# One unit in place of eight for the compressed attention branch of a recurrent mixer

## The reference

```python
k_cmp = compress(kc, pe_k, ck1, ck2)          # gelu(blk @ w1) @ w2, 15 blocks
v_cmp = compress(vc, pe_v, cv1, cv2)
s = jnp.einsum('bqhgd,bhcd->bhgqc', qb, k_cmp)
s = s - slopes[None, :, :, None, None] * jnp.abs(t[:, None] - cmp_end[None, :])
ok_c = cmp_end[None, :] <= t[:, None]
p_c = jax.nn.softmax(jnp.where(ok_c, s, NEG), axis=-1) * jnp.any(ok_c, axis=-1)[:, None]
o_c = jnp.einsum('bhgqc,bhcd->bqhgd', p_c, v_cmp)
...
return gb[..., 0:1] * o_c + gb[..., 1:2] * o_s + gb[..., 2:3] * o_w
```

## Time and profile before

| what | value |
|---|---|
| median of three runs (lowest to highest) | 1489.45 us (1488.96 to 1489.46) |
| profiled execution: its time, its span | 1488.83 us, 1486.7 us |
| granted TensorE clock, mean over the span | 0.992 |
| the doubling loop, from its first P to the tail's first product | about 130.7 to 228.2 us |

### The profile page before, as it was taken

How to read it: one execution, slowest core, us unless ns; L and a number is a source line. 1 busy time by engine, 2 the same in 40 slices (tenths; PEclk the granted TensorE clock), 3 DMA queues, 4 the chain that set the end, 5 groups by cost and what they waited for, 6 DMA issues and landing times.

```text
span 1486.7 us, 26239 instructions
## 1 busy us (share of the span) xinstructions
PE 1450.2 (98%) x10328; PEld 1332.9 (90%) x10328; DVE 958.1 (64%) x1577; ACT 706.2 (48%) x1159; POOL 86.9 (6%) x130
## 2 busy tenths in 40 slices
PE   8999999999999999999999999999999999999997
PEld 7887988899998999989988999999999878899997
DVE  4765545776666866666557666676666666676665
ACT  6753443544335434446665434354443656444342
POOL 2040001000002000010000000000000114000000
PEclk9999989999999999999999999999999999999999
DMA  8343000555453645433335555445454424355440
GB/s 343 145 149 128 1 2 1 199 217 203 174 195 110 238 180 202 179 128 128 128 128 221 204 187 193 176 165 211 170 200 182 147 89 163 136 209 205 171 169 29
DMA packets 26576, 238.07 MB, mean 160 GB/s; under 512 B 2544, under 2 KB 6784, under 8 KB 7808
## 3 DMA queue, kind: packets, MB, share of 16 engines
q1 hardware_dynamic: 23968, 233.65, 42.2%
q10 hardware_dynamic: 2528, 3.32, 0.7%
HBM read 235.89 MB, written 1.07 MB: 159 GB/s over the span
## 4 chain that ended last, share of the span: by engine, by line
PE 90%; DVE 5%; ACT 3%; issue 2%; POOL 1%; DMA 0%; ACTq 0%; DVEq 0%; POOLq 0%
PE ps L435 87%; DVE w_gu L1919 1%; PE ps L816 1%; DVE uT_l L1876 1%; PE ps L895 1%; DVE ring_r L1912 0%; DVE x L1938 0%; PE ps L439 0%; DVE ring_r L2270 0%; ACT uT_h L1241 0%; PE ps L1022 0%; DMA cst<-consts_in 0%; ACT wk L1419 0%; POOL small L1766 0%; POOL small L1767 0%
## 5 line engine op out<-in xcount | busy, mean ns | idle before, releaser
L435 PE MATMUL ps<-uT_h,w_gu 128*128 128x256 f32 x3520 | 614.3, 280 | 0.3
L435 PEld LDWEIGHTS ps<-uT_h,w_gu 128*128 128x128 f32 x3520 | 537.8, 188 | 11.1 <-issue 1.6
L435 PE MATMUL ps<-uT_l,w_gu 128*128 128x256 f32 x1760 | 478.8, 279 | 0.0
L435 PE MATMUL ps<-w_dn,h_r 128*128 128x512 f32 x1320 | 326.2, 396 | 2.1 <-issue 1.0
L435 PEld LDWEIGHTS ps<-uT_l,w_gu 128*128 128x128 f32 x1760 | 325.5, 188 | 0.0
L435 PEld LDWEIGHTS ps<-w_dn,h_r 128*128 128x128 f32 x1320 | 239.4, 188 | 53.3 <-issue 3.7
L1288 ACT CAST w_gu<-ring 128x2048 fp32r<-128x2048 f32 x110 | 209.9, 1909 | 156.3 <-PE ps L435 155.4
L1919 DVE TENSOR_TENSOR w_gu<-ring,w_gu 128x2048 fp32r<-128x2048 f32 x110 | 252.1, 2292 | 35.3 <-ACT w_gu L1288 35.3
L1949 DVE TENSOR_TENSOR us<-ps,bc 128x256 f32<-128x256 f32 x110 | 46.5, 423 | 202.9 <-PE ps L435 202.8
L1301 ACT ACTIVATE wk<-wk 128x256 f32<-128x256 f32 x110 | 46.1, 419 | 260.3 <-DVE wk L1947 260.3
L1294 ACT CAST w_dn<-ring 128x1024 fp32r<-128x1024 f32 x110 | 115.7, 1052 | 82.6 <-PE ps L435 82.4
(11 more groups left out here) (370 smaller groups left out, 1843.5 us busy)
## 6 DMA issues: line engine op xcount, KB each, us to landing
ring<-wstream SPq DMA_DIRECT2D x144, 1536.0 KB, 6.5
cst<-consts_in SPq DMA_DIRECT2D x1, 2185.0 KB, 13.7
wk<-t_row ACTq DMA_DIRECT2D x1, 2048.0 KB, 8.6
wk<-masks_in SPq DMA_DIRECT2D x1, 1216.0 KB, 23.4
x<-x_in SPq DMA_DIRECT2D x2, 512.0 KB, 4.5
ring<-wstream SPq DMA_DIRECT2D x1, 1024.0 KB, 9.0
inh<-gains ACTq DMA_DIRECT2D x2, 512.0 KB, 9.7
out_dram<-x SPq DMA_DIRECT2D x4, 256.0 KB, 2.2
```

Source lines behind the costliest of these rows:

```text
L435: return pe.matmul(o, l, r, start=start, stop=stop, skip_group_check=True)
```

## The change

The eight compressed units of a token tile become one unit that holds all eight heads. So there are 34 units in place of 48, in the same six groups, of 8, 1, 8, 8, 1 and 8 (the last unit of each is in `NSA_LAST` = 7, 8, 16, 24, 25, 33). For the merged unit:

- PE makes the scores of the two groups by four products of 32 columns, one for each pair of heads (j, j + 4), each with other weights; one transpose of 128 by 128; and one value product of 512 columns against `Vbd`, a block-diagonal tile that DVE builds once in `compress()` from the compressed values and a mask.
- DVE makes four operations of 128 columns in place of the fused one: sum, maximum over 16, difference, product with the slopes; and two steps later a sum over 16 for the denominators.
- ACT makes one plain exponential of 128 columns and one copy.

The steps are spread anew: `NSA_STEPS` is 1 and 2 in turn for q = 2 to 21 and 1 for q = 22 and 23, and the first step of a q is now always the one between P and dM. DVE's result follows four steps behind a group's last unit, `if i - 4 in NSA_LAST` (it was five). ACT's and PE's waits on `o_ready` go by the group, `a["pos"] == 0 and a["grp"] >= 2`. DVE's `compress()` moves from q = 4 to q = 2, and the constants grow by 16 columns.

```diff
-        hid = sb("hid", [P, 2, 2, 48])
+        hid = sb("hid", [P, 2, 160])
+        hid_k, hid_v = hid[:, :, 0:32], hid[:, :, 32:160]
         kcT = sb("kcT", [P, 2, 16])
-        vc = sb("vc", [16, 2, HD])
+        Vbd = inh[:, 2 * D:2 * D + 512].rearrange("p (u n) -> p u n", n=HD)
+        cmp_max = small[:, 64:72]
...
-        NSA_STEPS, CMP_FROM, BRANCHES = [0, 0] + [2] * 20 + [3, 3], 6, (1, 0, 2)
+        NSA_STEPS, CMP_FROM, BRANCHES = [0, 0] + [1, 2] * 10 + [1, 1], 6, (1, 0, 2)
...
-                    for b in BRANCHES:
+                    for n, b in enumerate(BRANCHES):
+                        grp = 3 * t + n
+                        if b == 0:
+                            units.append(dict(cmp=True, q=[qT[:, j, tk] for j in range(4)], K=P, grp=grp, pos=0, last=True,
+                                              dist=C("alibi_cmp", 16 * t, 16 * t + 16)))
+                            continue
                         for h in range(8):
                             g, slope = h // 4, 2.0 ** -(h + 1)
-                            u = dict(q=qT[:, h % 4, tk], scale=slope)
-                            if b == 0:
-                                u.update(k=kcT[:, g, 0:NC_CMP], K=NC_CMP, v=[vc[0:NC_CMP, g, :]],
-                                         dist=C("alibi_cmp", 16 * t, 16 * t + NC_CMP))
-                            else:
-                                kx, o = (ksT, kwT)[b - 1], (b - 1) * P + g * HD
-                                u.update(k=kx[:, g, 0:K], K=K, v=[vsw[:, kt, o:o + HD] for kt in range(t + 1)],
-                                         dist=C("alibi", P * (1 - t), P * (1 - t) + K))
-                            units.append(u)
+                            kx, o = (ksT, kwT)[b - 1], (b - 1) * P + g * HD
+                            units.append(dict(cmp=False, q=qT[:, h % 4, tk], scale=slope, grp=grp, pos=h, last=h == 7,
+                                              k=kx[:, g, 0:K], K=K, v=[vsw[:, kt, o:o + HD] for kt in range(t + 1)],
+                                              dist=C("alibi", P * (1 - t), P * (1 - t) + K)))
...
-                        pe.wait_ge(s["cmp_ready"], 2)
-                    for _ in range(NSA_STEPS[q] - 1):
+                        pe.wait_ge(s["kc_ready"], 1)
+                    for _ in range(min(NSA_STEPS[q], 1)):
...
-                    if NSA_STEPS[q]:
+                    for _ in range(NSA_STEPS[q] - 1):
...
-                    mm(ps[3 + i % 2][:, 0:a["K"]], a["q"], a["k"]).then_inc(s["S_ps"], 1)
+                    if a["cmp"]:
+                        for j in range(4):
+                            last = mm(ps[3 + i % 2][:, 32 * j:32 * j + 32], a["q"][j], kcT[:].rearrange("p g c -> p (g c)"))
+                        last.then_inc(s["S_ps"], 1)
+                    else:
+                        mm(ps[3 + i % 2][:, 0:a["K"]], a["q"], a["k"]).then_inc(s["S_ps"], 1)
                 if i >= 3:
                     u, a = i - 3, units[i - 3]
                     pe.wait_ge(s["npT_ev"], u + 1)
                     if u == 0:
-                        pe.wait_ge(s["gate_tok"], 2)
-                    if u % 8 == 0 and u >= 16:
-                        pe.wait_ge(s["o_ready"], u // 8 - 1)
-                    for k in range(0, a["K"], P):
-                        w = min(P, a["K"] - k)
-                        last = mm(ps[6 + u // 8 % 2][:, u % 8 * HD:(u % 8 + 1) * HD], nPT[0:w, u % 2, k:k + P],
-                                  a["v"][k // P], k == 0, k + P >= a["K"])
-                    last.then_inc(s["o_ps"], 1)
+                        pe.wait_ge(s["gate_tok"], 1)
+                        pe.wait_ge(s["cmp_v"], 1)
+                    if a["pos"] == 0 and a["grp"] >= 2:
+                        pe.wait_ge(s["o_ready"], a["grp"] - 1)
+                    o = ps[6 + a["grp"] % 2]
+                    if a["cmp"]:
+                        mm(o[:, :], nPT[:, u % 2, 0:P], Vbd.rearrange("p u n -> p (u n)")).then_inc(s["o_ps"], 1)
+                    else:
+                        for k in range(0, a["K"], P):
+                            last = mm(o[:, a["pos"] * HD:(a["pos"] + 1) * HD], nPT[:, u % 2, k:k + P],
+                                      a["v"][k // P], k == 0, k + P >= a["K"])
+                        last.then_inc(s["o_ps"], 1)
                 if 2 <= i < n + 2:
                     u, a = i - 2, units[i - 2]
                     pe.wait_ge(s["p_ready"], u + 1)
                     for k in range(0, a["K"], P):
-                        w = min(P, a["K"] - k)
-                        last = pe.transpose(ps[5][0:w, k:k + P], nPp[:, u % 3, k:k + w], ident)
+                        last = pe.transpose(ps[5][:, k:k + P], nPp[:, u % 3, k:k + P], ident)
...
-                    mm(ps[6][:, 0:30], C("ck2", half * P, (half + 1) * P), hid[:, 0, half, 0:30], half == 0, half == 1)
-                for g in range(2):
-                    for half in range(2):
-                        last = mm(ps[6][0:NC_CMP, 64 + g * HD:64 + (g + 1) * HD],
-                                  hid[:, 1, half, 15 * g:15 * g + 15], C("cv2", half * HD, (half + 1) * HD),
-                                  half == 0, half == 1)
+                    mm(ps[6][:, 0:32], C("ck2", half * P, (half + 1) * P), hid_k[:, half, :], half == 0, half == 1)
+                for half in range(2):
+                    last = mm(ps[5][:, 0:HD], hid_v[:, half, :], C("cv2", half * HD, (half + 1) * HD),
+                              half == 0, half == 1)
...
-                    if u % 8 == 0 and u >= 16:
-                        act.wait_ge(s["o_ready"], u // 8 - 1)
-                    act.activation(nPp[:, u % 3, 0:a["K"]], nSS[:, u % 3, 0:a["K"]], ACT.Exp, scale=-1.0,
-                                   bias=nmax[:, u % 4:u % 4 + 1],
-                                   accum_out=den[:, u % 16:u % 16 + 1]).then_inc(s["p_ready"], 1)
+                    if a["pos"] == 0 and a["grp"] >= 2:
+                        act.wait_ge(s["o_ready"], a["grp"] - 1)
+                    if a["cmp"]:
+                        act.activation(nPp[:, u % 3, 0:P], nSS[:, u % 3, 0:P], ACT.Exp).then_inc(s["p_ready"], 1)
+                    else:
+                        c = a["grp"] % 2 * 8 + a["pos"]
+                        act.activation(nPp[:, u % 3, 0:a["K"]], nSS[:, u % 3, 0:a["K"]], ACT.Exp, scale=-1.0,
+                                       bias=nmax[:, u % 4:u % 4 + 1],
+                                       accum_out=den[:, c:c + 1]).then_inc(s["p_ready"], 1)
                 if 2 <= i < n + 2:
                     u, a = i - 2, units[i - 2]
                     act.wait_ge(s["pT_ps"], u + 1)
                     if u >= 2:
                         act.wait_ge(s["o_ps"], u - 1)
-                    w, nn = min(P, a["K"]), P * -(-a["K"] // P)
-                    act.copy(nPT[0:w, u % 2, 0:nn], ps[5][0:w, 0:nn]).then_inc(s["npT_ev"], 1)
+                    act.copy(nPT[:, u % 2, 0:a["K"]], ps[5][:, 0:a["K"]]).then_inc(s["npT_ev"], 1)
...
-                    if q == CMP_FROM - 2:
+                    if q == 2:
                         compress()
-                    for _ in range(NSA_STEPS[q] - 1):
+                    for _ in range(min(NSA_STEPS[q], 1)):
...
-                v.wait_ge(s["o_ps"], 8 * (g + 1))
+                v.wait_ge(s["o_ps"], NSA_LAST[g] + 1)
                 V(v.reciprocal(rden, den[:, g % 2 * 8:g % 2 * 8 + 8]))
                 o = ps[6 + g % 2][:, :].rearrange("p (h n) -> p h n", h=8)
                 t, br = g // 3, BRANCHES[g % 3]
+                if br == 0:
+                    v.wait_ge(s["cmp_ready"], 2)
+                    rd = rden.rearrange("p (j g) -> p j g", g=2)
+                    V(v.tensor_tensor(rd, rd, gtok[:, t, 0:24:3].rearrange("p (g j) -> p j g", g=2), ALU.mult))
+                    V(v.tensor_tensor(obr.rearrange("p (g j) n -> p j g n", g=2),
+                                      o.rearrange("p (j g) n -> p j g n", g=2),
+                                      rd.unsqueeze(3).to_broadcast([P, 4, 2, HD]), ALU.mult))
+                    dst = onsa[:, t, :].rearrange("p (h n) -> p h n", h=8)
+                    V(v.tensor_tensor(dst, dst, obr, ALU.add), "o_ready")
+                    return
...
-                V(v.tensor_tensor_reduce(nSS[:, i % 3, 0:K], ps[3 + i % 2][:, 0:K], a["dist"], -a["scale"], 3e38,
-                                         ALU.add, ALU.min, nmax[:, i % 4:i % 4 + 1]), "max_ready")
-                if i % 8 == 4 and i > 8:
-                    nsa_result(i // 8 - 1)
+                if a["cmp"]:
+                    z = nSS[:, i % 3, 0:P].rearrange("p (u c) -> p u c", c=16)
+                    V(v.tensor_tensor(z, ps[3 + i % 2][:, 0:P].rearrange("p (u c) -> p u c", c=16),
+                                      a["dist"].unsqueeze(1).to_broadcast([P, 8, 16]), ALU.add))
+                    V(v.tensor_reduce(cmp_max, z, AX.X, ALU.max))
```

(30 more changed lines are left out.)

30 lines of the change are left out of this document (16 added, 14 removed).

## The result

The changed kernel takes **1491.85 us** (median of ten runs, 1489.99 to 1494.61). The kernel before, in runs of the same session, takes 1488.84 us (median of ten, 1480.50 to 1489.58). The ratio is 1.0053 with a 95% interval of 1.0036 to 1.0071: slower by 0.5%. The forecast was 1484.3 us.

What follows compares the result with a forecast made beforehand. The doubling loop was taken as bound by PE's own order of work; -7.5 + 0.7 + 6.0 - 6.8 + 2.5 = -5.1 us against 1488.83 gave 1483.7, as a median 1484.3 us. Range for 8 in 10: 1480.8 to 1490.0.

Steps and rivals of the forecast that it cites:

- The failed step: Tail behind the loop: its sequence stays as it was, so the loop's gain or loss simply shifts the end.
- PE's work, -7.5: Doubling loop: sixteen 15-column steps leave PE (-11.2 us), two merged units come (+3.7 us), together -7.5 us.
- the uncovered copy, +0.7: Loop, q = 7 to 10: shorter steps between P and dM no longer wholly cover ACT's copy, +0.7 us.
- Two stalls, 3.3 + 2.7 us: Loop, q = 9 and q = 20 to 21: PE waits for the merged transpose's copy behind DVE's result, 6.0 us.
- The rival in which they don't happen: Loop: PE never waits for `npT_ev` longer than now, giving 1475.8 us; chance 0.07.
- The clock, -6.8 us: Loop's last levels: 13.65 us at half clock should go, as 256-column steps now stand beside them, -6.8 us.
- -0.8 without the clock: Whole change: nearly all of the forecast gain is clock; without it the change is worth -0.8 us.
- New low stretches behind the stalls, +2.5 us: After PE's two waits: one and a half short low-clock stretches, +2.5 us, from none to +6.8.
- the rival of a tail at half clock: Clock falls in the second stall and stays low through the tail, +13.5 in place of 2.5: 1495.3 us; chance 0.10.
- The sum for the loop: Loop terms together: -7.5 + 0.7 + 6.0 - 6.8 + 2.5 = -5.1 us.
- those of "faster": Whole kernel: chance of being faster by over 0.2% (below 1486.5 us), stated as 0.62.
- those of "slower": Whole kernel: chance of being slower, beyond the 0.2% band, stated as 0.13.

Runs made afterwards that it cites:

- the two layouts of 1188.2 us: The kernel before with a 64-byte gap behind `wk` (1481.20 us), and with all tiles moved by 64 bytes (1480.78 us).
- the three kernels without them: Changed kernel with three sets of denominators: alone 1482.71 us; with new constants in their own tile, `wk` back in place, 1475.02; with `wk` moved 256 bytes, 1474.34.

## Why the prediction was wrong, by its own steps

**The failed step** is the sentence "Behind the loop the sequence of the tail is as it was, so what the loop gains or loses shifts the end." The loop's gain did shift the start of the layers, but their pace changed. The 16 more columns of constants were named among the changes and got no term at all. Their price is +8.8 us between the first cast and the last, and the run with 16 unused columns shows it without the rest of the change (+8.2 us against the two layouts of 1188.2 us; none of the three has a low clock from 690 to 710 us). With that term the sum would have been 1484.3 + 8.8 = 1493.1 us, 1.2 us over what was measured.

**PE's work, -7.5, and the uncovered copy, +0.7.** Right. From 129.90 us to the tail's first product PE is busy for 89.99 us in the kernel before with the gap behind `wk`, which has no low clock in the loop (up to 222.15 us), and for 82.52 us in the changed kernel (up to 221.72 us): -7.5 us. PE's waits for the copy of P went from 2.0 to 2.9 us: +0.9.

**Two stalls, 3.3 + 2.7 us.** Right in place, chain and size: 3.2 and 2.7 us, and the loop ends 5.8 us earlier when they are taken away. The rival in which they don't happen is out.

**The clock, -6.8 us.** Half right. Against the profiled execution of before the loop was 6.5 us shorter, and nearly all of this is the low clock: layouts of before with it have their first cast at 265.7 to 267.3 us, those without it at 259.2 to 261.4, and the changed kernel at 260.4. But 43 of 71 runs of the kernel before took under 1485 us, and the two layouts that were profiled at such a time (1481.20 and 1480.78 us) have no low clock in the loop, nor the one at 696 us. Against the first of them the tail's first product comes 0.4 us earlier in the changed kernel, where the prediction had -0.8 without the clock. So this gain is one against some runs of it, not against the kernel. The three times shown ahead of the prediction were all of the kind over 1488 us, and the prediction took one trace's stretch for a fixed cost. That the steps beside the last levels bear on it fits the runs: with tile 1's compressed branch moved away from them all 12 were under 1483 us.

**New low stretches behind the stalls, +2.5 us.** It did not come in the profiled execution; by the mean clocks, something of its size came in five of the changed kernel's ten runs. The profiled changed kernel has none in the loop; with `wk` in its old place one of 6.8 us stands at the second stall, and PE was busy 5.99 us of it at half clock, so 3.0 us. Of the 22 runs of the two kernels with the stalls 16 have a mean clock of 0.996 or less, of the 25 runs of the three kernels without them none, and the five such runs of the changed kernel lie some 3 us above its other five. Where in these runs the clock was low is shown by that one profile alone. It isn't the rival of a tail at half clock: the stretch of 222 to 246.7 us of the changed kernel has a clock of 1.00.

**The sum for the loop** was -5.1 us; between the two profiled executions it was -6.5. Behind it stand the layers with +8.8, and with 0.4 us for the mixer's tail and the last operations +2.7 us come out, as the two spans have it. The kernel is slower, but not by the clock in the stalls and the tail, which was the way that the prediction named: the profiled execution has full clock there and is slower all the same. The chances have a slip too: those of "faster" add up to 0.61 and those of "slower" to 0.14, where 0.62 and 0.13 are stated; nothing hangs on it.

**Left open:** by what mechanism in the memory or in TensorE's reads the distance acts; whether it is the distance to `uT` or to `yT`, since no run moved one of them alone (the products that read either slow down alike); and why the clock falls in some executions of a kernel and not in others.

## What to carry to other kernels

A tile that grows moves every tile behind it: an edit that "only" adds constants belongs into the sum, and where thousands of products stand behind it, a kernel with the same bytes added and nothing else is the first experiment. Look at the untouched part of the trace between two fixed marks (here the first and the last cast) before looking at the changed part. And take the spread of many runs of the kernel before, not of three, before a stretch of one trace is booked as a gain.

## What the runs showed of the hardware

Products of 256 columns whose weights and moving operand stand in SBUF at another distance of each other take 118.3 to 119.9 ns in place of 116.7 from start to start, at moves of 32, 64, 128 and 160 bytes, and 116.8 again at 256. It is 8 to 13 us of 1190 in these layers. The Trainium skill, "TensorE: Matmul & The Clock Gate", section "Step-by-step: what each phase is for", says that "Loading the next tile's weights doesn't steal SBUF read bandwidth from the running matmul", by two independent read ports. The stretch between the casts, 1188.2 us at one distance and 1201.0 at another with the same instructions, shows that the place of the operands matters by 1%, and the products are as slow beside idle ACT and DVE; that the two reads of TensorE meet is a guess which would fit it, and no run here shows it.

The clock of TensorE fell to 0.50 for 13.7 us with PE busy throughout, in four of the layouts of the kernel before and not in the others, at 210.2 to 212.3 us each time. Ahead of that stand products of 15 columns or rows among those of 64. Two pauses of PE of 3.2 and 2.7 us brought no low clock in the profiled changed kernel, and in another layout of the same products 6.8 us of it, from within the second pause. By the mean clock of the runs (0.993 to 0.996 in 16 of 22 runs with the pauses, 0.997 or more in all 25 without them) such pauses seem to bring the clock down in most executions and not in all; one profile alone shows it happen in the pause.
